# One further identity matmul per tick on TensorE in the first half-layer of a two-layer encoder trunk

## The reference, cut to what matters

```python
for l in range(DEPTH):
    mod = cond @ ada_w[l] + ada_b[l]
    sh_m, sc_m, g_m, sh_f, sc_f, g_f = jnp.split(mod[:, None, :], 6, axis=-1)
    h = rms_norm(x, norm_mix_g[l]) * (1.0 + sc_m) + sh_m
    y = mixer_ab(h, ...) if l % 2 == 0 else mixer_c(h, ...)
    x = x + g_m * y
    h = rms_norm(x, norm_ffn_g[l]) * (1.0 + sc_f) + sh_f
    x = x + g_f * peer_ffn(h, peer_w_q[l], peer_sub_keys[l], peer_u[l], peer_v[l])
return rms_norm(x, final_norm_g)
```

## Time and profile before

| | |
|---|---|
| median of 3 runs | 3510.07 us |
| profiled execution, its time | 3502.65 us |
| profiled execution, span of the trace | 3500.9 us |
| PE busy | 2827.6 us (81%) |
| DVE busy | 2324.6 us (66%) |
| ACT busy | 1150.5 us (33%) |
| POOL busy | 1145.6 us (33%) |
| mean granted TensorE clock | 0.913 |
| mean DMA rate | 356 GB/s |

### The profile page before, as it was taken

The page is one execution under the profiler, slowest core; times in us unless marked ns, Lnnn a source line. Parts: engine busy times, 40 slices in busy tenths (PEclk is TensorE's granted clock), DMA queues, the critical chain, the costliest instruction groups (busy, mean ns, idle before and its releaser), DMA issues. The chain is left out here.

```text
span 3500.9 us, 29698 instructions
## 1 busy us (share of the span) xinstructions
PE 2827.6 (81%) x8552; PEld 1556.8 (44%) x8552; DVE 2324.6 (66%) x5492; ACT 1150.5 (33%) x3413; POOL 1145.6 (33%) x1065
## 2 busy tenths in 40 slices
PE   4787788788979869887889869887888877777776
PEld 2465443455555426544444327444444432233222
DVE  6774788637758975576588865675688954445444
ACT  1131233327723231362233332572233322322222
POOL 0000244312222233223344443333344443344332
PEclk9857999999989989878999999888999999999999
DMA  7663799967789899889999999888999999999997
GB/s 271 249 239 113 278 421 417 387 232 276 267 328 377 293 386 390 316 318 361 419 419 411 399 402 413 330 327 334 399 418 418 408 398 421 421 416 407 421 422 329
DMA packets 272765, 1247.28 MB, mean 356 GB/s; under 512 B 19925, under 2 KB 114517, under 8 KB 141399
## 3 DMA queue, kind: packets, MB, share of 16 engines
q0 software_dynamic: 153792, 1098.97, 77.8%
q1 hardware_dynamic: 118802, 146.35, 11.8%
q10 hardware_dynamic: 8, 0.06, 0.0%
HBM read 1243.18 MB, written 7.36 MB: 357 GB/s over the span
## 5 line engine op out<-in xcount | busy, mean ns | idle before, releaser
L1421 PE MATMUL psum<-space 128*128 128x512 f32 x3564 | 1774.6, 637 | 447.4 <-ACT space L1454 406.6
L1528 POOL DMA_INDIRECT space<-in_peer_uv,expert x1024 | 1127.5, 1101 | 2072.0 <-PE psum L1421 1501.9
L1480 DVE CUSTOM_DVE_ANT_0 space<-space,h 128x1024 f32<-128x1024 f32 x1024 | 1248.4, 1223 | 803.5 <-DMA space<-in_peer_uv,expert 750.2
L1421 PEld LDWEIGHTS psum<-space 128*128 128x128 f32 x3564 | 680.4, 200 | 1290.2 <-ACT space L1454 614.6
L1443 ACT ACTIVATE space<-space 128x2 f32<-128x2 f32 x512 | 103.8, 203 | 1564.2 <-DVE space L1480 1562.8
L594 PE MATMUL psum<-space 128*128 128x256 f32 (+2 forms) x1840 | 444.2, 401 | 71.5 <-DMA space<-in_w_in_c 28.4
L594 PEld LDWEIGHTS psum<-space 128*128 128x128 f32 x1840 | 364.8, 201 | 168.7 <-issue 69.8
L1454 ACT ACTIVATE space<-ident,space 128x128 f32<-128x128 f32 x891 | 308.6, 386 | 0.5 <-PE psum L1421 0.4
L1115 PE MATMUL psum<-space 128*128 128x256 f32 x1024 | 266.0, 388 | 7.1 <-ACTq L460 6.9
L1115 PEld LDWEIGHTS psum<-space 128*128 128x128 f32 x1024 | 198.3, 195 | 141.4 <-issue 115.7
L1446 ACT ACTIVATE space<-space,gate 128x1 f32<-128x1 f32 x1024 | 245.6, 287 | 16.8
(11 more groups left out here) (163 smaller groups left out, 1616.8 us busy)
## 6 DMA issues: line engine op xcount, KB each, us to landing
space<-in_peer_w_q SPq DMA_DIRECT2D x32, 1024.0 KB, 15.6
space<-in_ada_w SPq DMA_DIRECT2D x12, 2048.0 KB, 15.7
space<-in_ada_w POOLq DMA_DIRECT2D x12, 2048.0 KB, 8.5
space<-in_w_in_c SPq DMA_DIRECT2D x24, 1024.0 KB, 19.3
space<-in_peer_uv,expert POOLq DMA_INDIRECT x1024, 10.1
space<-in_w_in_ab SPq DMA_DIRECT2D x14, 1024.0 KB, 13.7
space<-in_w_out_ab SPq DMA_DIRECT2D x8, 1024.0 KB, 7.6
space<-skewed SPq DMA_DIRECT2D x32, 256.0 KB, 6.6
```

The lines of the kernel that those rows point to most:

```text
L1421: last = nc.tensor.matmul(b.bank[part][:, :], b.diag2[:, n % DIAGS, :], b.pairs[:, p % PAIRS, 1, part * BANK:(part + 1) * BANK], start=(p ...
L1480: dve.tensor_tensor_reduce(out=row, in0=row, in1=b.h[:, tile(q), :], scale=1.0, scalar=0.0, op0=ALU.mult, op1=ALU.add, accum_out=b.dots2[: ...
L1528: pool.indirect_dma_start(out=b.pair_rows[q % PAIRS], out_offset=None, in_=ins["peer_uv"], in_offset=bass.IndirectOffsetOnAxis(ap=b.expert ...
```

## The change

From the first tick of the latents to the last but one of the second norm (ticks 33 to 144 of the lead), PE issues after each tick one matmul more: the identity as weights, the mask of 128x512 as the moving operand, into bank 0. Nothing waits for it and nothing reads it, and the matmuls of the gathers begin their sums in bank 0 anew. It stands in PE's own program, so that it is ahead of the next tick's instructions on PE, and those issued after a part's last tick are ahead of PE's drain at that part's end.

```diff
         def _(pe):
             ticks = stream(pe, "pe", parts, gate)
             taken = 0
+            idle_from, idle_to = ticks_in(lead[:3]), ticks_in(lead)
             while taken < plan.lead:
                 next(ticks)
                 taken += 1
+                if idle_from < taken < idle_to:
+                    nc.tensor.matmul(b.bank[0][:, :], b.ident[:, :], b.causal[:, :], start=True, stop=True)
```

## The result

The changed kernel has a median of 3520.09 us over 10 runs (3512.35 to 3531.78), the kernel before 3507.23 us over 10 runs beside it (3488.86 to 3526.61). The ratio is 1.0045, with a 95% interval of 1.0023 to 1.0066. The prediction gave 3525 us for the median, in a range from 3500 to 3565. The profiled execution took 3528.43 us.

A forecast was written before the change was run, and what follows sets the result against it. PE was taken to bound attention (half clock) and the output projection (full clock), DVE the head transposes. Terms 2 + 2.5 + 3 + 2.5 + 4.5 + 3 - 1.5 gave +16 us, a median of 3525 us, range 3500 to 3565.

The forecast's parts named there:

- the output projection: Lead's output projection: PE already sets the pace at 2.4 GHz, so nine added matmuls cost time; +4.5 us.
- Attention: Lead's attention: full clock nearly pays for 52 added matmuls, pairs of 3.4 and 3.9 us; +3 us (-4 to +9).
- the ramp ticks: Four ramp ticks of attention also get their matmul, 3.6 us, of which DVE's tail hides half.
- my lower bound: Price of one added matmul at full clock: 0.88 to 1.02 us, taken as 0.90.
- the head transposes: Lead's head transposes: two more matmuls per two groups make PE the bound, 28.5 us against 25.8; +2.5 us.
- The second norm: Lead's second norm: transposes start at half clock after 5 us idle, three matmuls between their groups; +3 us (+1 to +5.4).
- The choice: Expert choice after the second norm: starts at full clock where its first matmuls ran at half; -1.5 us.
- one to one: Gathers start once the lead has chosen experts, so a shift of the lead's end passes unchanged to the kernel's end.
- The full clock: From latent heads to end of attention: full clock expected, with at most 2 us between two added matmuls.
- the clock stays at half: Rival: clock not released in attention, perhaps also head transposes; +105 to +145 us, say 3635 us; chance 0.09.
- The fall after an idle time: Transposes after the head norm: PE idle some 5 us, so half clock expected there, within that part's +2.5 us.
- The faster rival: Rival: full clock throughout, matmuls fall into waits, attention at DVE's 75 us; -29 us, 3481 us; chance 0.07.

The follow-up runs named there:

- twelve further profiled executions: Profiles of the follow-up kernels, all doing the same work behind the first gather; that rest took between 3097 and 3144 us.
- attention only: The changed kernel with its 512-column matmul kept in attention's ticks alone; latents to first gather 244.2 us (+2.7), attention 98.5 us.
- narrow then wide: Against the kernel before, in attention only: 512 columns in 6 ticks, 128 through tick 17, then 512; latents to first gather 298.7 us (+57.2), attention 153.8.
- the burst: As narrow then wide to tick 17, then four 512-column matmuls back to back in tick 18, 128 columns after; latents to first gather 228.9 us (-12.7), attention 84.2.

## Why the prediction was right

**The size.** The forecast for a like execution was +16 us, the stretch shows +13.1 and the medians +12.9. The reading that carried it was that PE is busy 10.00 of 10 us in attention and in the output projection, so that the clock has to pay for what raises it, and that it nearly pays: 1.8 to 2.0 us added to a pair, and about 1.6 to 1.9 taken off it by the full clock. Attention was priced at +3 and measured +2.9, and so close a hit is luck: the pairs cost 2.9 (8 x 0.18 + 16 x 0.09) where I had about 1, and the ramp ticks nothing where I had 1.8.

**The terms.** Where an added matmul has neighbours of full height it costs 0.86 us, less than the 0.90 that I took and even than the 0.88 of my lower bound. This and the other instructions, shorter too than I read them (0.22 us for the transposes of a group where I had 0.25; 3.46 for 16 instructions of the output projection where I had 3.5), made the head transposes +1.2 instead of +2.5 and the output projection +3.8 instead of +4.5. Beside 32-row scores it costs 1.00, near the upper bound of 1.02, and the rest of that pair took 2.03 where I read 2.1. The pairs came out as 3.38 and 4.05, priced at 3.4 and 3.9. The second norm was taken at +3 and cost +3.4; both rises after the long idle times of DVE's work came as read (1.92 us for the first matmul in the transposes). The choice gave back 2.0 of an expected 1.5, but not for the reason that I gave. It is as short (41.85 to 41.87 us) in eleven of the twelve further profiled executions, and seven of these have no added matmul in the second norm. So these 2 us may not belong to the change at all.

**The rest of the kernel.** The first gather moved from the latents by 13.1 us, and the time behind it stayed within the scatter of all kernels. The step "one to one" is consistent with that; at +-20 us of scatter in single executions it is the timed medians that bear it out, to within their interval.

**The clock.** The full clock came as forecast, but the reason that I gave was only half right. I read from the second half that such matmuls raise the clock, and took it that 2 us between two of them would do. The rise there came with two of them in a row (four instructions, 3.09 us). Interleaved one to a tick, they raise it beside the latent heads (attention only: by 193 us) and didn't beside the 32-channel maps (narrow then wide). What saved the change is the order of events: attention began with the clock up, and no gap of PE opened behind it. The rival "the clock stays at half" was 0.09 in my chances and 105 to 145 us in its price; a kernel with the same matmul beside nearly all of the 32-channel maps, but a gap ahead of them, pays 57 us. I had no term for such a gap. The fall after an idle time, ahead of the transposes, came as forecast (4.74 us idle, then 1.92 us for a matmul), though one of the two rows that I read it from doesn't show it: at 287.40 the clock had been at half all through attention.

**The faster rival.** It needed the matmuls to fall into waits, and in this form they don't. A like gain is there all the same, for smaller matmuls: DVE's pace, 75 us by my estimate, is reached to within 5 us (80.4) once the clock is up and is kept with 128 columns. The Trainium skill's advice on idle gaps (TensorE: Matmul & The Clock Gate, "Why this matters for your kernels") points the right way in that form only; here the fall in the kernel without matmuls behind tick 20 came with PE busy 2.00 of 2 us, so busy time by itself isn't what keeps the clock.

## What to carry to other kernels

Filler work for the clock is worth only what the stage has beyond it: read which engine is next (here DVE at 1.4 us per tick), and make the filler so small that this engine sets the pace, instead of adding to the engine that is the bound. Put it only where the clock is low while PE is the bound; where the clock is full already it costs its whole length, and where another engine is the bound it costs what doesn't fit into the waits (together 10.2 of the 13.1 us here). Look for the gap that a faster stage opens (a late DMA of some side work), since one idle stretch can lose the clock for the rest of the stage, and keep a short uninterrupted burst ready behind it.

## What the runs showed of the hardware

The clock has a memory in this kernel. With one matmul of 512 columns per tick beside the 32-row score maps it stayed at 1.00 for 65 us where it had come in high, and at 0.50 for 110 us where it had come in low, with PE busy 10.00 of 10 us in both. Four of these matmuls back to back brought it from 0.50 to 1.00 within 5.7 us. Transposes brought it up among the latent heads' ticks. And it was lost with PE busy throughout: by 228 us when nothing wide stood between the 32-channel maps, and likewise with matmuls of 64 columns between them, while 128 columns kept it in each of the two profiled executions of that kernel and in that of the burst. All kernels but that with 128 columns behind tick 20 were profiled once. The runs don't separate the 32 rows of the scores from all else in which the ticks of the maps differ from those of the latent heads, and whether fewer than four matmuls back to back would do beside the maps wasn't tried.
